# Building the dispatch lists of a 16-expert MoE layer: the slot lists, the tile counts, the number of rounds and the first round

## What is computed

```
pg    = softmax(h32 @ w_route_group + b_route_group);  g_idx = argmax(pg)      # 4 groups
le_g  = the 4 expert logits of that group
top_p, top_i = top_k(softmax(le_g), 2)                                         # 2 of 4 experts
wts   = g_w * top_p / sum(top_p);   e_idx = g_idx * 4 + top_i
for each expert e (16):  y_e = (silu(xb @ w_gate[e]) * (xb @ w_up[e])) @ w_down[e]
y[token] += y_e[slot of the token] * wts
y_final  = rmsnorm(x + y)
```

## Time and profile before

| | |
|---|---|
| median of 3 runs | 1412.17 us (1408.61 to 1413.27) |
| profiled execution, its time | 1416.3 us |
| its span, first to last instruction | 1414.5 us |
| TensorE busy | 1264.5 us, 89% of the span |
| VectorE, ScalarE, GpSimd busy | 467.6, 356.1, 279.8 us |
| mean granted clock of TensorE | 0.952 |

### The profile page before, as it was taken

The page is one execution under the profiler, slowest core; times in us unless marked ns, Lnnn a source line. Parts: engine busy times, 40 slices in busy tenths (PEclk is TensorE's granted clock), DMA queues, the critical chain, the costliest instruction groups (busy, mean ns, idle before and its releaser), DMA issues. The chain is left out here.

```text
span 1414.5 us, 28157 instructions
## 1 busy us (share of the span) xinstructions
PE 1264.5 (89%) x12448; PEld 902.5 (64%) x12448; DVE 467.6 (33%) x903; ACT 356.1 (25%) x722; POOL 279.8 (20%) x159
## 2 busy tenths in 40 slices
PE   6999999988999888878799998589999999999990
PEld 4666655555666677666544454378887888788760
DVE  4103554266554656765341112501111101101113
ACT  3113544344452343424131112010011011101103
POOL 0000000011011799993000000012111211121010
PEclk9999999999999999999999998589999999999995
DMA  6312000101103100022303112927887788788717
GB/s 209 95 45 64 15 1 16 30 19 34 30 19 35 27 4 4 4 48 66 109 16 141 60 59 75 349 75 245 272 301 260 254 278 299 243 266 283 273 19 265
DMA packets 95259, 173.61 MB, mean 123 GB/s; under 512 B 19096, under 2 KB 41043, under 8 KB 94756
## 3 DMA queue, kind: packets, MB, share of 16 engines
q1 hardware_dynamic: 87476, 151.12, 31.7%
q0 software_dynamic: 7680, 20.98, 6.3%
HBM read 146.65 MB, written 26.44 MB: 122 GB/s over the span
## 5 line engine op out<-in xcount | busy, mean ns | idle before, releaser
L620 PE MATMUL ps<-arena 128*128 128x355 f32 x960 | 297.7, 466 | 1.9 <-issue 1.7
L1188 PEld LDWEIGHTS ps<-arena 128*128 128x128 f32 x2048 | 280.0, 191 | 6.9 <-issue 6.9
L1188 PE MATMUL ps<-arena 128*128 128x160 f32 x2048 | 283.9, 301 | 0.6 <-DVE arena L2060 0.6
L620 PEld LDWEIGHTS ps<-arena 128*128 128x128 f32 x960 | 179.7, 190 | 110.9 <-issue 13.4
L1088 PE MATMUL ps<-arena 128*128 128x512 f32 (+1 forms) x288 | 130.6, 603 | 0.7 <-DVE arena L1881 0.7
L1202 PE MATMUL ps<-arena 128*128 128x512 f32 x256 | 114.1, 599 | 0.7 <-DVE arena L2065 0.7
L2200 POOL DMA_INDIRECT arena<-h_dram,idxA x16 | 16.1, 1005 | 471.8 <-DVE idxB L2095 267.8
L2065 DVE TENSOR_TENSOR arena<-arena,ps 128x160 f32<-128x160 f32 x64 | 20.5, 321 | 265.3 <-ACT arena L1573 265.3
L1573 ACT ACTIVATE arena<-ps 128x160 f32<-128x160 f32 x64 | 19.4, 304 | 337.1 <-PE ps L1188 337.1
L1088 PEld LDWEIGHTS ps<-arena 128*128 128x128 f32 (+1 forms) x288 | 51.4, 183 | 66.6 <-issue 64.8
L2143 POOL TENSOR_TENSOR arena<-arena 128x1024 f32<-128x1024 f32 x4 | 11.4, 2856 | 377.3 <-DVE arena L1695 377.3
(11 more groups left out here) (352 smaller groups left out, 1755.8 us busy)
## 6 DMA issues: line engine op xcount, KB each, us to landing
arena<-in_w_exp_gate SPq DMA_DIRECT2D x16, 2048.0 KB, 12.5
arena<-in_w_exp_up SPq DMA_DIRECT2D x16, 2048.0 KB, 17.4
arena<-in_w_exp_down SPq DMA_DIRECT2D x16, 2048.0 KB, 21.9
arena<-in_w_in SPq DMA_DIRECT2D x16, 512.0 KB, 3.9
arena<-in_x_prompt SPq DMA_DIRECT2D x9, 512.0 KB, 4.0
h_dram<-arena SPq DMA_DIRECT2D x8, 512.0 KB, 2.6
x_dram<-arena SPq DMA_DIRECT2D x8, 512.0 KB, 3.6
out_y_prompt<-arena SPq DMA_DIRECT2D x8, 512.0 KB, 6.2
```

The source lines that it names most:

```text
L620: last = pe.matmul(ps[:, q % 2, 0:m], wr[:, n % 3, k, :], hT[:, k, a:a + m], start=(k == 0), stop=(k == KB - 1))
L1188: last = pe.matmul(ps[:, 3 + f % 2, n * CAP:(n + 1) * CAP], w[a][:, k, f * P:(f + 1) * P], xgT[:, a, k, :], start=(k == 0), stop=(k == KB ...
```

## The change

Five things are changed, all between the logits and the final norm.

1. **Tile counts by one product.** `OHs[:, 0:128]` as stationary operand times a column of ones gives the counts of tiles 0 to 7 in one column; ScalarE copies it to `tcol`; TensorE then multiplies `tcol`, broadcast, with a constant 0/1 matrix `prefix` (loaded by a new 72 KB DMA) and adds the result onto the rank in PSUM. VectorE reads the finished rank from PSUM. The two copies and the loop over tiles are gone. `valid` is multiplied into the 36 columns of `ohg` once, and no longer into the two matrices of 144.
2. **One-hot rows as moving side.** `hot` now has room for all 18 m. VectorE fills it with five `tensor_tensor` instructions (of 2, 4, 4, 4, 4 m). `OHX[m]` (48 columns) is the stationary operand, `hot` (160 columns) the moving one; even m go to columns 0 to 47 of the array, odd m to columns 64 to 111. The two sums lie in PSUM on partitions 0 to 47 and 64 to 111; VectorE and ScalarE copy one each to `slots`, and five small products with two stacked unit matrices add them and turn them, so that PSUM holds what it held before.
3. **Number of rounds later.** Its 15 instructions now stand behind the making of `rowB`. The total counts come from a third product and a copy by ScalarE.
4. **First round ahead of the loop.** Round 0 is plain code on every engine; only then do the engines load `nround` and enter the loop over rounds 1 to 6. Each index list has its own signal to GpSimd.
5. **End.** SyncE goes through the loop first and waits for `round_done` behind it.

The diff, cut to its core:

```diff
+    prefix = ((e[:, None] % NE == u[None, :] % NE) & (e[:, None] // NE < u[None, :] // NE)) * 1.0
...
-        hot = part(R0, 2 * CAP).rearrange("p (s r) -> p s r", s=2)
+        slots = part(R0, CAP)
+        tcol = part(R0 + CAP, 1)
...
+        hot = part(4 * D, 2 * NTT * CAP).rearrange("p (m r) -> p m r", m=2 * NTT)
+        HOTS = [(0, 2), (2, 6), (6, 10), (10, 14), (14, 18)]
...
+            sp.dma_start(rt_["tot"], i["c_prefix"]).then_inc(s["shift_in"], 16)
...
+            sp.wait_ge(s["round_done"], rounds)
+            alone(sp)
...
             pe.wait_ge(s["r_dve"], 3)
-            pe.matmul(ps[:, 7, 0:NTT * NE], T["strict"], rt_["OHs"], start=True, stop=True)
-            pe.matmul(ps[:, 7, NTT * NE:2 * NTT * NE], T["ones"], rt_["OHs"], start=True, stop=True).then_inc(s["r_pe"], 1)
+            pe.matmul(ps[:, 6, 0:1], rt_["OHs"][:, 0:P], T["ones"][:, 0:1], start=True, stop=True).then_inc(s["r_pe"], 1)
+            pe.matmul(ps[:, 7, 0:NTT * NE], T["strict"], rt_["OHs"], start=True, stop=False)
+            pe.wait_ge(s["r_act"], 3)
+            pe.wait_ge(s["shift_in"], 48)
+            pe.matmul(ps[:, 7, 0:NTT * NE], tcol.to_broadcast([P, P]), rt_["tot"], start=False, stop=True).then_inc(s["r_pe"], 1)
+            pe.matmul(ps[:, 4, 0:NTT * NE], T["ones"], rt_["OHs"], start=True, stop=True).then_inc(s["r_pe"], 1)
...
-                    for m in range(2 * NTT):
-                        pe.wait_ge(s["hot"], 2 * NTT * r + m + 1)
-                        rhs = OHX[:, m].rearrange("p a e -> p (a e)")
-                        pe.matmul(ps[:, 7, 0:3 * NE], hot[:, m % 2, 0:P], rhs, start=(m == 0), stop=(m == 2 * NTT - 1))
-                        for j in range(TQ):
-                            last = pe.matmul(ps[j * XB:(j + 1) * XB, 6, 0:3 * NE], hot[:, m % 2, P:CAP], rhs,
-                                             start=(m == 0), stop=(m == 2 * NTT - 1), tile_position=(0, j * XB))
-                        last.then_inc(s["hot_ps"], 1)
...
+                for k, (a, b) in enumerate(HOTS):
+                    pe.wait_ge(s["hot"], NHOT * r + k + 1)
+                    for m in range(a, b):
+                        c = HD * (m % 2)
+                        last = pe.matmul(ps[c:c + 3 * NE, 5, 0:CAP], OHX[:, m].rearrange("p a e -> p (a e)"), hot[:, m, :],
+                                         start=(m < 2), stop=(m >= 2 * NTT - 2), tile_position=(0, c))
+                last.then_inc(s["hot_ps"], 1)
+                pe.wait_ge(s["hot"], NHOT * r + NHOT)
...
+                two = T["eye64"][:, 0:3 * NE]
+                pe.matmul(ps[:, 7, 0:3 * NE], slots[:, 0:P], two, start=True, stop=True).then_inc(s["hot_ps"], 1)
+                for j in range(TQ):
+                    last = pe.matmul(ps[j * XB:(j + 1) * XB, 6, 0:3 * NE], slots[:, P:CAP], two, start=True, stop=True, tile_position=(0, j * XB))
+                last.then_inc(s["hot_ps"], 1)
...
-            for t in range(NTT):
-                link(dve.tensor_tensor(rank[:, t, :], rank[:, t, :], X["cnt"], ALU.add))
-                link(dve.tensor_tensor(X["cnt"], X["cnt"], tot[:, t, :], ALU.add))
...
+                for a, b in HOTS:
+                    n = b - a
+                    dve.tensor_tensor(hot[:, a:b, :], T["iota"][:, None, :].to_broadcast([P, n, CAP]), X["rk"][:, a:b][:, :, None].to_broadcast([P, n, CAP]),
+                                      ALU.is_equal).then_inc(s["hot"], 1)
+                dve.wait_ge(s["hot_ps"], 3 * r + 1)
+                dve.tensor_copy(slots[0:3 * NE, :], ps[0:3 * NE, 5, 0:CAP]).then_inc(s["hot"], 1)
+                dve.wait_ge(s["hot_ps"], 3 * r + 2)
+                dve.tensor_copy(idxA[:, :], ps[:, 7, 0:NE]).then_inc(s["i_ok"], 1)
```

More of the change, by code:

```diff
@@ L1209, in down, with one_round @@
                 last.then_inc(s["ya_ps"], 1)
+            def one_round(r, later):
+                for k, (a, b) in enumerate(HOTS):
[6 more added lines that the diff above has]
+                pe.wait_ge(s["hot"], NHOT * r + NHOT)
+                if not later:
+                    pe.wait_ge(s["r_act"], 4)
+                two = T["eye64"][:, 0:3 * NE]
[3 more added lines that the diff above has]
+                last.then_inc(s["hot_ps"], 1)
+                pe.wait_ge(s["i_ok"], 2 * r + 2)
+                g0 = NE * r
+                turn(g0, 0, True)
+                gate_up(g0, 0, True)
+                turn(g0 + 1, 1, False)
+                down(g0, 0, True)
+                gate_up(g0 + 1, 1, False)
+                with pe.Fori(1, NE // 2) as q:
+                    g = NE * r + 2 * q
+                    turn(g, 0, False)
+                    down(g - 1, 1, False)
+                    gate_up(g, 0, False)
+                    turn(g + 1, 1, False)
+                    down(g, 0, False)
+                    gate_up(g + 1, 1, False)
+                down(g0 + (NE - 1), 1, False)
@@ L1241, in _ @@
+                    pe.wait_ge(s["round_done"], r)
                     alone(pe)
+                    one_round(r, True)
         @block.scalar
@@ L1560, in _ @@
             act.activation(rt_["m2"], rt_["m2"], ACT.Exp).then_inc(s["r_act"], 1)
+            act.wait_ge(s["r_pe"], 1)
+            act.copy(tcol, ps[:, 6, 0:1]).then_inc(s["r_act"], 1)
+            act.wait_ge(s["r_pe"], 3)
+            act.copy(rt_["rank"], ps[:, 4, 0:NTT * NE]).then_inc(s["r_act"], 1)
             def turned(g, a):
@@ L1996, in _ @@
             link(dve.memset(lg[:, NT, :], 0.0))
+            link(dve.memset(slots, 0.0))
             dve.wait_ge(s["g_lg"], NTT)
@@ L2011, in _ @@
             first_max(leg, X["m1"], oh1, oh2)
+            link(dve.tensor_tensor(by("ohg", 4), by("ohg", 4), wide(T["valid"], 4), ALU.mult))
             link(dve.scalar_tensor_tensor(leg, oh1, -1e30, leg, ALU.mult, ALU.add))
@@ L2203, in _, with one_round @@
             pool.wait_ge(s["h2o1"], 32 * 4)
+            def one_round(r, later):
+                pool.wait_ge(s["i_ok"], 2 * r + 1)
+                for e in range(NE):
+                    if e >= 2:
+                        pool.wait_ge(s["xb_ps"], NE * r + (e - 1))
+                    alone(pool)
+                    gather(xgA[:, e % 2, :], h2_dram, idxA[:, e:e + 1]).then_inc(s[f"xg{e % 2}"], 16)
+                    if e == 0:
+                        pool.wait_ge(s["i_ok"], 2 * r + 2)
+                        alone(pool)
+                    gather(xgB[:, e % 2, :], h2_dram, idxB[0:XB, e:e + 1]).then_inc(s[f"xg{e % 2}"], 16)
+                    if e == 2:
+                        pool.wait_ge(s["s_ok"], r + 1)
+                    if e >= 3:
+                        scatter(r, e - 3)
+                for e in range(NE - 3, NE):
+                    scatter(r, e)
+                pool.wait_ge(s["yst0"], 16 * NE * (r + 1))
+                pool.wait_ge(s["yst1"], 16 * NE * (r + 1))
+                pool.nop().then_inc(s["round_done"], 1)
@@ L2204, in _ @@
+            one_round(0, False)
             pool.wait_ge(s["n_rounds"], 1)
             rounds = pool.value_load(nround[0:1, 0:1], min_val=1, max_val=ROUNDS)
[L2206 removed]
+            with pool.Fori(1, ROUNDS) as r:
                 with pool.If(rounds > r):
[L2208 to L2224 removed]
```

179 lines of the change are left out of this document (77 added, 102 removed).

## The result

| | before | after |
|---|---|---|
| median | 1412.72 us (4 runs, 1408.61 to 1417.74) | 1393.25 us (4 runs, 1391.76 to 1394.72) |
| profiled span | 1414.5 us | 1392.4 us |
| TensorE busy, mean clock | 1264.5 us, 0.952 | 1258.9 us, 0.954 |

The ratio is 0.9851, 95% interval 0.9825 to 0.9877. The kernel is 19.5 us faster by the medians; 21.1 had been predicted, as 1391.1 us with a range of 1385 to 1398. One execution of c2, the run further down that has part 5 alone, took 2486.8 us and is left out of its median and ratio.

What follows compares the result with a forecast made beforehand. The path to the first gathered rows was taken as the bound, since experts then follow without a gap on TensorE. Gains 18.0 + 3.1 = 21.1 us; 1412.2 - 21.1 = 1391.1 us, range 1385 to 1398.

Steps and rivals of the forecast that it cites:

- Part 1: Routing chain up to the first slot comparison: it starts at 891.6 instead of 900.68 us.
- Part 2: Slot lists: comparisons 3.7 us, paired products 5.4 us; idxA ends at 898.8, 19.0 us earlier than before.
- Part 3: Gathers: second lands 5.0 us after issue; TensorE starts turning at 906.1 instead of 924.10, 18.0 us earlier.
- the scatters' 9.5: Median scatter time in us, taken as the upper bound for a gather in a full weight stream.
- Part 4: First experts: turn, gate_up and the rest follow as before, the first 6 us at half clock.
- rival C: Slot products raise the clock: lists 1.6 us sooner, turn and gate_up save 1 + 1.4; up to 4 us; chance 0.12.
- Part 5: End: SyncE's walk through six unneeded rounds moves ahead of its wait; 3.31 us becomes 0.2, 3.1 us earlier.
- 905 to 907: Sign of the forecast: time in us at which the first gather's rows are turned.
- limit of 911: Turned rows at 911 us mean mild A; starting outside 904 to 911 makes the prediction wrong.
- B: Rival: slot products run one after the other, costing 4.5 us, 1395.6; mild A or B, or both, 0.18.
- D: Rival: weights become the expert loop's limit, kernel slower, 1420; 0.04 shared with slightly longer loop or no change.
- A: Rival: gathers wait behind weights; full 1405, chance 0.04; mild 4.5 us less gain, 1395.6, 0.18 shared with B.

Runs made afterwards that it cites:

- c2: Kernel before with only the new end: SyncE passes unneeded rounds first, then waits for the final signal; median 1418.6 us, ratio 1.0005.
- e4: Kernel after, but the 15 instructions for the number of rounds stand ahead of the slot comparisons again; median 1396.8 us, ratio 0.9862.
- e3: Kernel after, but all 18 slot products go to the same 48 array columns, one after the other; median 1398.0 us, ratio 0.9855.
- e1: Kernel after, but expert 1's weights are issued only once the first gathered rows have landed; median 1393.1 us, ratio 0.9823.
- f1: Kernel after, but TensorE, VectorE and ScalarE wait for the final signal before passing the loop; median 1397.7 us, ratio 0.9881.
- c3: Kernel after with expert 1's weights held until the first rows land and 44 unused slot products in the wait; median 1392.5 us, ratio 0.9841.
- g1: Kernel after with 62 unused slot products in the wait for gathered rows, weights not held; median 1393.1 us, ratio 0.9853.
- c1: Kernel after, unchanged, run once more; 1395.4 us (6 runs), ratio 0.9870.
- f2: c3 with TensorE, VectorE and ScalarE waiting for the final signal before passing the loop; median 1391.7 us, ratio 0.9843.
- e2: Kernel after with 46 unused slot products on TensorE while it waits for gathered rows; median 1399.8 us, ratio 0.9886.

## Why the prediction was right

**Part 1, the routing chain: right.** First comparison 10.4 us after the first weights' issue instead of 19.4, 9.1 earlier; 9.1 was worked out. The new wait of VectorE for the rank cost nothing: 2081 follows the instruction ahead of it without a gap. The number of rounds is hidden, as said, and e4 gives its price without the cover, 3.0 us.

**Part 2, the slot lists: right.** From the first comparison to the end of `idxA` 7.05 us instead of 17.11, so 10.1 less; 9.9 was worked out. The products took 5.24 us (5.4 predicted), all at 0.50, the comparisons 3.43 in all. e3 shows the overlap on which that rests. The first gather came 19.1 us earlier, counted from the first weights; 918.77 against 899.7, also 19.1, had been worked out.

**Part 3, the gathers: right in kind, too small.** The step that failed is the 5.0 us from the second gather's issue to its landing, "the nearest kind of transfer": it took 6.7 to landing and 6.9 to use. The bound of 5.0 came from gathers that met the last part of one expert's stream (expert 2's third matrix landed at about 981.3, 3 us behind the issue of the gather at 978.37); here all three matrices of expert 1 were still to land, at about 909, 914 and 921. The true value lies between 5.0 and the scatters' 9.5. The price is 1.9 us of the 21.1, and e1 shows the cause. The gather was issued at 899.19, behind those matrices (884.85, 887.35 and 895.14), and landed at 905.9, ahead of all three, so here it didn't wait for what was queued before it.

**Part 4: right for the first expert, 0.3 to 0.8 us short for the rest.** C is the same within the scatter of the clock (0.4 us longer in the first pair of traces, 0.3 shorter in the second). Of rival C's first half little came true: the clock rose, but only as the slot products ended (896.3 against 895.45 in after), so the lists gained nothing by it, and up to 0.4 us in f1, c3 and g1, where it rose 4.3 us after the first of them and they took 4.84 to 4.86 us. The second half did not come true: the clock was lost while TensorE waited (899.8 in after, 895.8 in c1), as was held against it. D grew by 0.3 and 0.8, at the last scatter; this give-back was not foreseen.

**Part 5: right.** 3.31 us became 0.14; predicted 3.1 less, measured 3.2, in the trace (c2's times don't show it). Not foreseen: 1.3 to 1.6 us from the end. By f1 and f2 they come from the engines' walk being out of the way of the loads (F is 27.7 and 28.6 us with the walk beside them); e2 and c3 show that the gain isn't there each time.

The sum by the two first traces: 9.1 + 10.1 - 3.0 - 0.4 - 0.3 + 3.2 + 1.6 = 20.3, against 20.2 counted from the first issue (-0.4 is column C). Term for term, 1.9 us too much for the gather, 0.4 for column C and 0.3 for the last scatter stand against 1.6 too little at the end. That the total missed by only 0.9 us is in part luck: the shorter end that made up for the gather was not foreseen. It is luck, too, that the first turn, at 906.05, lies in the 905 to 907 named as a sign: the first weights went out 2.0 us earlier than in the trace before, and on that trace's time the turn is at 908.0, outside 905 to 907 and inside the limit of 911. B and D did not show, and of A only a part of its mild form, 1.9 us of 4.5.

## What to carry to other kernels

When a serial chain is shortened, ask what will then run beside its last step: here the gathers moved from idle DMA engines (share 0.00 in the 1.5 us ahead of the second gather) into a weight stream (1.05), and paid 3 us for it. Holding back the weights that are needed last gave the gather its 3 us back, and the counted stretch 1.7; no gain in the time was shown. Work that only prepares a loop which mostly isn't entered can be moved off the path at its full price, 3.0 us here. Taking the first round out of the loop leaves a walk past a body never run, 6.3 us here and 10.0 beside other loads, so it should be passed while something else is waited for. To tell 3 us in a kernel whose runs differ by 10, count from the last point that all versions share.

## What was not expected of the hardware

- Instruction streams that are alike up to 880 us, but for one small load and a memset, reached that point between 875.7 and 885.0 us. The single times of a kernel spread as widely. What causes it was not looked into.
- The second gather, of 128 KB, took 3.9 us from issue to use in before, where the DMA share was 0.00 ahead of it and 0.77 from its issue to its use, and 6.9 in after, beside a stream of weights that kept the share at 1.05.
- ScalarE's walk through six unused rounds took 4.0 us where it had just run the loop's body, 6.3 where it never had, and 10.0 where it never had and the loads of `x_dram` ran beside it (5.7 of them at the first jump over the body, f1 and f2).
- The granted clock rose 4.3 to 6.1 us after the first of 18 products of 128 x 48 x 160 (6.1 in after, 5.1 in c1, 4.3 in c3, g1 and f1), where 90 products with 48 moving columns had left it at 0.50 for 16.5 us. In the wait behind, of 2.6 us (e2) or 9.3 us (after), it was lost; with the wait filled it was kept twice over the turn (c3 and f2, at most 0.22 us idle ahead of it), while in g1, with 0.55 us of waiting, it fell 1.5 us behind the turn's end.
